# Hybrid SSD, HGRN2 and expert layer in fp32: the gated heads' projections as pairs by Strassen's seven block products

## The reference

```python
z_l, xbc_l, dtr_l, qr_l, fr_l, ir_l, og_l, gm_l, gh_l = jnp.split(hl @ w_in, splits, axis=-1)
...
qh = jax.nn.silu(q)
log_f = jnp.log(lb + (1.0 - lb) * jax.nn.sigmoid(fz))
k = (1.0 - lb) * jax.nn.sigmoid(-fz)
...
q_l, k_l, lf_l, v_l = hg_split(raster_to_cols(qr_l, rows), raster_to_cols(fr_l, rows), raster_to_cols(ir_l, rows))
o = gla_scan(make_dirs(q_c, q_l, q_c, q_l), ...)
...
oh = rms_norm(oh, g_hg_norm) * jax.nn.silu(og)
```

## Time and profile before

| | us |
|---|---|
| median of 3 runs (lowest to highest) | 1856.69 (1856.19 to 1856.93) |
| span of the profiled execution | 1854.0 |
| PE busy | 1745.3 (94%) |
| DVE busy | 810.5 (44%) |
| ACT busy | 486.2 (26%) |
| POOL busy | 394.9 (21%) |

### The profile page before, as it was taken

One profiled execution on the slowest core, in us unless ns is written; L12 is line 12 of the kernel. 1 busy time (PEld: TensorE's weight loads), 2 busy tenths in 40 slices (PEclk: granted clock), 3 DMA queues, 4 the chain that ended last, 5 costly groups with the idle time before them and its releaser, 6 DMA issues.

```text
span 1854.0 us, 19751 instructions
## 1 busy us (share of the span) xinstructions
PE 1745.3 (94%) x7472; PEld 1027.3 (55%) x7472; DVE 810.5 (44%) x1330; ACT 486.2 (26%) x847; POOL 394.9 (21%) x472
## 2 busy tenths in 40 slices
PE   5999999999999999999999999999898887988887
PEld 2555555555556777677766478885533333333332
DVE  4626555464457556456555687663330000000004
ACT  3221422414233443434443200002321101111012
POOL 2114142240436433444334000000010000010000
PEclk9999999999999999999999999999899998999989
DMA  7221323212321111111113344467679999999996
GB/s 303 95 80 57 114 68 97 76 55 68 103 68 35 46 46 45 45 34 45 45 34 103 125 136 137 135 229 266 272 309 429 430 430 429 429 392 429 430 425 246
DMA packets 153697, 340.17 MB, mean 183 GB/s; under 512 B 15430, under 2 KB 105759, under 8 KB 140826
## 3 DMA queue, kind: packets, MB, share of 16 engines
q1 hardware_dynamic: 135760, 315.26, 44.9%
q10 hardware_dynamic: 13114, 15.89, 2.6%
q0 software_dynamic: 4752, 8.05, 1.1%
HBM read 331.44 MB, written 16.99 MB: 188 GB/s over the span
## 4 chain that ended last, share of the span: by engine, by line
PE 88%; DMA 6%; DVE 3%; issue 2%; ACT 1%; SPq 0%; DVEq 0%; ACTq 0%
PE bank L774 12%; PE bank L522 12%; PE bank L2713 11%; PE bank L1835 10%; PE bank L815 6%; PE bank L2731 6%; PE bank L527 5%; PE bank L518 3%; PE bank L1877 3%; PE bank L1386 3%; DMA stay<-in_w_up_dram 2%; DMA stay<-in_w_down_dram 2%; PE bank L859 2%; DMA arena<-in_w_up_dram 2%; PE bank L867 1%
## 5 line engine op out<-in xcount | busy, mean ns | idle before, releaser
L774 PE MATMUL bank<-stay,arena 128*128 128x512 f32 (+1 forms) x704 | 240.0, 496 | 0.0
L2713 PE MATMUL bank<-arena 128*64 128x512 f32 x832 | 188.2, 609 | 14.3 <-ACT arena L2616 6.2
L774 PEld LDWEIGHTS bank<-stay,arena 128*128 128x128 f32 x704 | 132.4, 190 | 99.7 <-issue 92.3
L522 PE MATMUL bank<-arena 128*128 128x512 f32 x384 | 168.9, 592 | 0.0
L1256 POOL TENSOR_TENSOR arena<-arena 128x256 f32<-128x256 f32 x112 | 87.6, 782 | 269.3 <-DVE arena L1509 155.2
L2713 PEld LDWEIGHTS bank<-arena 128*64 128x64 f32 x832 | 66.4, 140 | 131.4 <-issue 119.1
L2731 PE MATMUL bank<-arena 128*64 128x512 f32 x416 | 107.3, 675 | 32.3 <-issue 18.8
L522 PEld LDWEIGHTS bank<-arena 128*128 128x128 f32 x384 | 71.7, 190 | 83.7 <-issue 83.7
L815 PE MATMUL bank<-arena,stay 128*128 128x512 f32 x256 | 114.6, 595 | 2.2 <-DVE arena L1067 2.2
L2854 DVE TENSOR_TENSOR arena<-arena,bank 128x512 f32<-128x512 f32 x17 | 11.7, 688 | 237.5 <-PE bank L2713 237.5
L1528 DVE TENSOR_TENSOR arena<-arena 128x256 f32<-128x256 f32 x112 | 59.0, 567 | 106.1 <-ACT arena L1287 73.0
(11 more groups left out here) (456 smaller groups left out, 2800.5 us busy)
## 6 DMA issues: line engine op xcount, KB each, us to landing
arena<-in_w_gate_dram SPq DMA_DIRECT2D x24, 2048.0 KB, 18.0
arena<-in_w_down_dram SPq DMA_DIRECT2D x24, 2048.0 KB, 23.3
arena<-in_w_up_dram SPq DMA_DIRECT2D x22, 2048.0 KB, 22.9
arena<-in_w_in_dram SPq DMA_DIRECT2D x58, 512.0 KB, 3.8
arena<-in_w_ada_dram SPq DMA_DIRECT2D x12, 2048.0 KB, 10.5
stay<-in_w_gate_dram SPq DMA_DIRECT2D x8, 2048.0 KB, 22.9
stay<-in_w_up_dram SPq DMA_DIRECT2D x8, 2048.0 KB, 17.2
arena<-in_w_in_dram ACTq DMA_DIRECT2D x6, 2048.0 KB, 9.7
```

The lines of the kernel that those rows point to most:

```text
L522: mm = pe.matmul(b[:, :], w[:, k, :], src[:, k, 0:LAT], start=(k == 0), stop=(k == KT - 1))
L774: mm = pe.matmul(ps[:, 0:n], w[:, k, :], hT[:, k, o:o + n], start=(k == 0), stop=(k == KT - 1))
L2713: mm = pe.matmul(b[cols, :], xgT[r][:, k, cols], w[u][:, k, :], start=(k == 0), stop=(k == KT - 1))
```

## The change

- `hTp` and its copies go. POOL makes four sums of token blocks (`tok_t`, each 4 k-tiles x 256 tokens) after all scalings.
- For heads 1 to 7 the latent projections of the two `f` are one product of (2 x 128 channels) by 512 tokens over 1024, done in 2 x 2 blocks by seven block products of 4 matmuls of 256 columns, 28 in all in place of 16 of 512. `q` and `og` are a second such pair. Head 0 keeps plain units, in raster order; ACT's copy turns the order.
- Two block products that are to be added share a half bank. DVE adds the rest: `f_sums`, `f_last_sum`, `q_sums`, `q_last_sum`, most of them with the result in column order. POOL adds weight blocks (4 x 512 columns a pair) into the place of `ysT`'s first 8 tiles; these are written to DRAM in group 2 (2 MB) and read back in body 6.
- Values are made with channels on partitions (8 matmuls of 512 and 8 of 256), copied by ACT in column order, turned by six transposes (`turn_v`) and copied into `Vh` by ACT (`v_rows`). POOL's copy goes. Contexts of both `f` are one step, `f_context`.
- The output gate's sigmoid moves into `head_gates`, and `output_gate` near the body's start. `hg_sync` loads by the new events, and the merge's first loads follow them.

The diff, cut; `by_column` and `by_row` are views of the token order.

```diff
-            for k in range(KT):
-                pool.wait_ge(s_hl, KT + k + 1)
-                pool.tensor_copy(hTp[:, k, :]..., hT[:, k, 0:LAT]...).then_inc(s_hp, 1)
+            pool.wait_ge(s_hl, 2 * KT)
+            pool.tensor_tensor(tok_t[0], of_h["12"], of_h["11"], ALU.subtract).then_inc(s_hp, 1)
...
                     decay_rows(g, h)
+                    if g == 2 and h == 2:
+                        sp.wait_ge(s_ys, START + 8)
+                        sp.dma_start(ys_dram, stay[:, 0:8 * LAT]).then_inc(s_spill, 16)
...
+        def turn_v(pe, h):
+            pe.wait_ge(s_pev, copied(h - 1, V_CONTEXT_COPY))
...
+            for i in range(NCH):
+                mm = pe.transpose(bank[4 + i // 4][:, i % 4 * P:(i % 4 + 1) * P], pV[:, i * P:(i + 1) * P], ident[:, :])
+        def block_product(pe, b, half, w, t, opens=False, ends=False):
+            for k in range(4):
+                mm = pe.matmul(b[:, half * HALF:(half + 1) * HALF], w[:, k, :], t[:, k, :], start=(opens and k == 0), stop=(ends and k == 3))
+        def f_opens(pe, h):
...
+            block_product(pe, bank[0], 0, wh[0][:, 0:4, :], of_h["11"], opens=True)
+            block_product(pe, bank[0], 1, wh[0][:, 4:8, :], of_h["21"], ends=True).then_inc(s_pu, 1)
+            pe.wait_ge(s_pev, copied(h - 1, V_CONTEXT_COPY))
+            block_product(pe, bank[1], 0, fsum[S3], tok_t[2], opens=True)
+            block_product(pe, bank[1], 1, fsum[S1], tok_t[0], ends=True)
+            pe.wait_ge(s_pev, copied(h, F_U1))
+            block_product(pe, bank[0], 0, fsum[S2], tok_t[1], opens=True)
+            block_product(pe, bank[0], 1, fsum[S4], of_h["22"], ends=True).then_inc(s_pu, 1)
...
+        def q_sums(dve, own, h):
+            dve.wait_ge(s_pev, copied(h, Q_U1))
+            own.link(dve.tensor_tensor(by_column(pq, 0), by_row(u1), by_row(u12[:, HALF:LAT]), ALU.add))
+            dve.wait_ge(s_pu, projected(h, Q_MIDDLE))
+            own.link(dve.tensor_tensor(u1, u1, bank[0][:, 0:HALF], ALU.add))
+            own.mark(dve.tensor_tensor(u3, u1, bank[1][:, 0:HALF], ALU.add))
+            own.link(dve.tensor_tensor(by_column(pq, 1), by_row(u1), by_row(bank[1][:, HALF:LAT]), ALU.add))
+            dve.tensor_tensor(pog[:, HALF:LAT], u3, bank[1][:, HALF:LAT], ALU.add)
+            dve.tensor_tensor(by_column(pq, 1), by_column(pq, 1), by_row(bank[0][:, HALF:LAT]), ALU.add).then_inc(s_half, 1)
+        def q_weight_sums(pool, h):
+            pool.wait_ge(s_wh[2], 16 * h + 32)
+            pool.wait_ge(s_wh[3], 16 * h + 32)
...
+            pool.tensor_tensor(qsum[S1], w21, w22, ALU.add).then_inc(s_wsum, 1)
...
+                    v_unit(pe, 0, 0)
...
+                    v_unit(pe, 0, 1)
+                    f_opens(pe, 0)
                     turn_y(g, True)
-                    head_unit(pe, 1, 2)
+                    f_ends(pe, 0)
...
                     dve.tensor_scalar(yt[:, cc, :], yt[:, cc, :], rst[:, cc:cc + 1], None, ALU.mult).then_inc(s_yn, 1)
-                if not last:
+                if last:
+                    f_sums(dve, own, 0)
+                else:
...
                 merge(0)
+                if not first and not last:
+                    f_sums(dve, own, h)
                 for i in range(2, NL):
                     operand(i)
+                    if i == 5 and not last:
+                        q_sums(dve, own, h)
                     merge(i - 1)
+                    if i == 2 and not last:
+                        f_last_sum(dve, h)
...
+                if sums:
+                    pool.wait_ge(s_pu, projected(h, F_LAST))
+                    f_weight_sums(pool, h + 1)
+                    pool.wait_ge(s_pu, projected(h, Q_LAST))
+                    q_weight_sums(pool, h + 1)
```

More of the change, by code:

```diff
@@ L530, in head_unit_copy, with by_column @@
[L530 to L537, removed]
+        def by_column(v, half=None):
+            w = v.rearrange("p (w r) -> p r w", r=ROWS)
+            return w if half is None else w[:, half * ROWS // 2:(half + 1) * ROWS // 2, :]
@@ new lines, in by_row, with first_head_unit, first_head_copy @@
+        def by_row(v):
+            return v.rearrange("p (r w) -> p r w", w=GRID_W)
+        def first_head_unit(pe, u):
+            w, b = wh[UW[u]], bank[u % 2]
+            pe.wait_ge(s_wh[UW[u]], 16)
+            pe.wait_ge(s_pev, START + u - 1)
+            n, o = (CTX, LAT) if u in (1, 3) else (LAT, 0)
+            for k in range(KT):
+                mm = pe.matmul(b[:, 0:n], w[:, k, :], hT[:, k, o:o + n], start=(k == 0), stop=(k == KT - 1))
+            mm.then_inc(s_pu, 1)
+        def first_head_copy(act, u):
+            act.wait_ge(s_pu, u + 1)
+            b = bank[u % 2]
+            if u in (1, 3):
+                ins = act.copy(pf[u // 2][:, LAT:T], b[:, 0:CTX])
+            elif u == 5:
+                ins = act.copy(pog, b[:, :])
+            else:
+                dst = pq if u == 4 else pf[u // 2][:, 0:LAT]
+                ins = act.copy(by_column(dst), by_row(b[:, :]))
+            ins.then_inc(s_pev, 1)
@@ new lines, in v_unit, with v_copy @@
+        def v_unit(pe, n, part):
+            pe.wait_ge(s_wh[4], 16 * n + 16)
+            b, cols, o = bank[part], CTX if part else LAT, LAT if part else 0
+            for k in range(KT):
+                mm = pe.matmul(b[:, 0:cols], wh[4][:, k, :], hT[:, k, o:o + cols], start=(k == 0), stop=(k == KT - 1))
+            mm.then_inc(s_pu, 1)
+        def v_copy(act, n, part):
+            act.wait_ge(s_pu, projected(n - 1, V_LATENT + part))
+            if part:
+                act.copy(pV[:, LAT:T], bank[1][:, 0:CTX]).then_inc(s_pev, 1)
+            else:
+                act.copy(by_column(pV[:, 0:LAT]), by_row(bank[0][:, :])).then_inc(s_pev, 1)
@@ new lines, in f_context, with f_ends @@
+        def f_context(pe, h):
+            pe.wait_ge(s_wh[0], 16 * h + 32)
+            pe.wait_ge(s_wh[1], 16 * h + 32)
+            pe.wait_ge(s_vc, h + 1)
+            for d in range(2):
+                for k in range(KT):
+                    mm = pe.matmul(bank[4][:, d * CTX:(d + 1) * CTX], wh[d][:, k, :], hT[:, k, LAT:T], start=(k == 0), stop=(k == KT - 1))
+            mm.then_inc(s_fx, 1)
+        def f_ends(pe, h):
+            pe.wait_ge(s_half, summed(h, F_OPEN_SUMS))
+            block_product(pe, bank[1], 0, wh[1][:, 4:8, :], tok_t[3], opens=True, ends=True).then_inc(s_pu, 1)
@@ L1376, in hg_tensor @@
         def hg_tensor(pe):
-            def unit(h, last, u):
-                if not last:
-                    head_unit(pe, h + 1, u)
             def level(h, i):
@@ L1390, in body @@
             def body(h, first, last):
-                if not first:
-                    unit(h, last, 0)
+                if not first and not last:
+                    f_opens(pe, h)
                 if last:
@@ L1680, in build @@
         no_rows = arena[:, 0:D]
-        HALF = LAT // 2
         UNITS = 5
```

285 lines of the change are left out of this document (195 added, 90 removed).

## The result

The changed kernel takes 1891.38 us in the median of 4 runs (1891.13 to 1893.33), the kernel before 1856.44 beside it: ratio 1.0194, 95% interval 1.0180 to 1.0208. That is 34.9 us slower, where 4.9 were forecast and 1873 was the upper end. The sign was right, the size wrong by a factor of seven.

What follows compares the result with a forecast made beforehand. TensorE was taken as the bound (88% of the chain of waits); start -1.7, entrance and body 0 +9.5, bodies 1 to 6 -2.4, body 7 -0.5 gave +4.9 on 1856.7, so 1861.6 us, range 1844 to 1873.

Steps and rivals of the forecast that it cites:

- part C: Bodies 1 to 6: fewer matmul columns, but a new 2.5 us wait before level 5; 60.0 becomes 59.6, in all -2.4 us.
- rival 2: Bodies 0 to 5: POOL's q and og weight sums slow DVE's gates, PE waits 1 to 2 us; 1867 to 1874, chance 0.15.
- DVE has long been waiting there: Bodies 1 to 6: DVE already waits when the middle products end, since operand 5 follows level 3's product, one slot earlier.
- rival 3: The clock falls in each body after the wait, costing 1.7 us more; 14 us more in all, 1875, chance 0.09.
- part A: Program start: without POOL's hT copies beside DVE's scalings, PE's first projection takes 6.87 for 8.72 us; lasting gain, -1.7 us.
- The spill and its load: Writing 2.1 MB in group 2 and loading it back from body 6: both taken at 0, at worst +3 us.
- Part B: Entrance and body 0: keys wait for head 1's sums, level 0 at 588.0 instead of 579.72; +9.5 us, bounds +4 and +12.
- Part D: Body 7: transposes +0.7, but the output gate's table load and the 1.18 us wait behind it go; -0.5 us.
- Rival 1: The wait at level 5 doesn't come: 1844.1, chance 0.14; without the entrance's idle and slow clock either, 1828, chance 0.03.

Runs made afterwards that it cites:

- run 1: Changed kernel with GpSimd's weight sums for heads 2 to 7 cut to 8 of 128 columns per k-tile (part of the computation left out): 1869.49 us.
- run 9: Changed kernel with one wait more: GpSimd's f weight sums of the next head wait for operand 5; 1869.42 us, ratio 1.0070.
- run 5: Changed kernel with the edits of run 1 and run 4 together, level 4's matmuls done three times: 1860.75 us.
- run 4: Changed kernel with level 4's four matmuls done six times in bodies 0 to 6, same result, to fill TensorE's wait: 1880.60 us.
- Run 3: Changed kernel with VectorE's f sums of head 1 behind head 0's running sums instead of ahead of head 0's keys: 1882.38 us.
- run 10: run 6 plus head 1's f sums and seventh product standing in body 0 as in the other bodies: 1850.91 us, ratio 0.9975.
- run 6: Changed kernel with TensorE's chunk states moved from before level 3 to between levels 4 and 5 in bodies 0 to 6: 1857.56 us, ratio 1.0007.
- run 2: Changed kernel with GpSimd's f weight sums of the next head waiting until VectorE has done the q sums: 1884.80 us.
- run 11: run 10 plus merge 4 ahead of the q sums and ScalarE's context values' copy ahead of level 0's exponentials: 1854.15 us, ratio 0.9991.
- run 7: Changed kernel with GpSimd's f weight sums at the start of the body using them, and level 0's exponentials behind three ScalarE copies: 1889.68 us.
- run 8: run 6 and run 7 together, plus q weight sums inside the body and head 1's f sums and seventh product in body 0: 1865.43 us, ratio 1.0058.

## Why the prediction was wrong

**The step that failed** is part C: "DVE needs five sums, 1.92, with two in column order 0.4, and the merge 0.72", with a wait of 2.5 us and bounds of 1.75 and 3.0. It measured 4.65. The mechanism, its place and its undisturbed size were right (2.21 in body 6 and run 1, 2.23 in run 9). Two terms were missing.

- *POOL's f weight sums.* I placed the q weight sums beside the gates (rival 2) and asked what they cost there. I never placed the f weight sums, which follow the last level differences and fall on operand 5 and the first q sum. They make DVE 2.4 us late for the sums that the wait is made of: 4.65 for the 2.21 without them, where 2.5 was forecast. Run 9, which moves them by one wait, takes off 22 us, run 1 the same. The sentence "DVE has long been waiting there" was wrong by them: DVE was still in operand 5.
- *The clock.* Behind 4.65 us of waiting PE worked at half rate until 2.9 us were lost. I had this as rival 3, with a chance of 0.09, and held it off because 2.5 lay under the 3.08 of the earlier trace rows. It came true, but priced too low: 2.0 us a body, where the wait and the clock together took 5.05 over the forecast. Runs 1 and 5 show that even 2.21 us cost 1.7 in five bodies of six, run 4 that with the real wait filled no clock is lost. In the kernel before, a wait of 1.43 us (at 527.50, before L815) left the clock at 1.00, and the one of 3.08 didn't. The range between was open, and I should have priced 2.5 as undecided.

Together: 5 x (2.15 + 2.9) = 25.3 us against the forecast, and 2.2 of the same kinds in body 0. At the end of the heads 28.3 us lie between forecast (+4.9) and result (+33.2); part A's missing 1.1 makes up the rest.

**Part A** gave 1.6 at first, as worked out; DVE scales in 3.74 us and PE's first projection takes 7.05. "PE is the bound behind it, so the gain lasts" failed: by 548 us 1.0 was given back, all of it before SSD products (L1044) at 201.1, 316.7 and 433.2 us. Each waits for DVE, whose product ahead (L1232, both inputs in SBUF) takes 1.17, 1.34 and 0.95 beside POOL's additions (L729), and took 0.69, 0.94 and 0.80 before, where DVE and POOL met at other moments. It looks like the same contention; no run tries it. **The spill and its load** cost nothing that shows: no wait on them stands in PE's list. **Part B** was right to 0.3 us at its entrance: its times leave part A out, so 0.6 is to be added to the measured ones, which gives 571.6 for the keys (571.6 forecast) and 587.7 for level 0 (588.0). Run 3 shows that the order of the sums makes it, and run 10 that it can be mended. **Part D** was right: body 7 is 0.6 shorter, and no wait stands before the merge's first product. **Rival 1** (no wait) lost, though run 6 made nearly that of it. **Rival 2** did not decide in the changed kernel: in bodies 1 to 5 the keys stayed ahead of POOL (1.14), and the running sums that were slowed had slack. It decided in runs 2 and 11, at 1.2 to 1.6 us of wait ahead of the outputs.

The Trainium skill (SBUF — State Buffer, "SBUF: two separate sides") says that a DVE instruction with two inputs in SBUF and a GpSimd one that reads SBUF take a port pair in turn, each for its whole length. I weighed it as a rule that speaks against the change, and gave it 0.15 at the wrong place. The traces agree with it: beside POOL, operations with both inputs in SBUF took 1.68 for 0.61 and 1.80 for 0.68, and those with one in PSUM 0.42 and 0.72 as ever. In body 2 four DVE instructions ran beside POOL's four sums, and each came out 0.9 to 1.1 us longer.

## What to carry to other kernels

When work moves to GpSimd, list what VectorE does in each stretch in which that work can run, for every instruction of it: here each instruction with all its inputs in SBUF lost 0.9 to 1.1 us beside GpSimd's sums of 1.27 us, and those that read PSUM lost nothing. A wait of TensorE of 2 us or more, repeated in a loop, can have two prices, itself and the clock behind it; what helped most here was independent work of TensorE moved into it, ten matmuls for 34 us.

## What the runs showed of the hardware

- After 2.20 to 2.23 us of waiting before level 5 the granted clock fell in five of bodies 1 to 6 in run 1 and in run 9 and in three of them in run 7, with the same work ahead of each, and not in body 6 of the changed kernel. After 1.94 us (run 8) it fell in one body of five, after 1.00 us in none. Each fall cost 1.7 us. What tells the bodies apart stays open.
- Useless matmuls in a wait made the kernel faster: 1891.4 to 1880.6 us.
- GpSimd pays as well: its sum of 512 columns takes 1.26 to 1.31 beside VectorE operations that read PSUM (run 9) and 1.45 to 1.72 beside those that don't; in the changed kernel one beside a scan takes 2.8.
- VectorE's keys (L1683; one input tensor, in SBUF) are held up too: 3.03 and 2.91 for 1.14 in runs 2 and 11.
- An addition of 256 columns takes 0.61 with an input or output in column order and 0.42 without.
